# One rounding and one splitting instruction per weight slab in a 16-stage fp32 transformer block on one core

## The reference, cut to what matters

```python
mod  = silu(c) @ w_mod + b_mod                        # 2048 x 6144, for c and c_ctx
proj = hx @ w_in ; proj_c = hc @ w_in[:, k and v]     # 2048 x 8192, 256 tokens and 256 context tokens
...two attentions (differential with rope; neighbourhood)...
h    = h + gate * (concat(oa, ob) @ w_out)            # 2048 x 2048
proj = layernorm(rmsnorm(h)) @ w_in_2                 # 2048 x 7184: conv branch, q, k, v, o, gates
...conv gate, mLSTM cell...
h    = layernorm(ALPHA * h + mix @ w_out_2)
q    = h @ peer_wq ; top-16 of 128 keys twice, top-16 of 256 pairs
act  = gelu(h @ u.T)                                  # all 16384 experts, then masked to the chosen ones
ff   = (gate * act) @ v                               # 16384 x 2048
out  = layernorm(ALPHA * h + ff)
```

## Time and profile before

| | |
|---|---|
| median of 3 runs | 3272.75 us |
| profiled execution, first to last instruction | 3268.1 us |
| PE busy | 2988.1 us (91%) |
| DVE busy | 1825.0 us (56%), of it w_lo at L153 1264.5 us |
| ACT busy | 1490.0 us (46%), of it w_hi at L146 1145.7 us |
| loads | 944 x 512 KB, mean 159 GB/s |

### The profile page before, as it was taken

The page is one execution under the profiler, slowest core; times in us unless marked ns, Lnnn a source line. Parts: engine busy times, 40 slices in busy tenths (PEclk is TensorE's granted clock), DMA queues, the critical chain, the costliest instruction groups (busy, mean ns, idle before and its releaser), DMA issues. The chain is left out here.

```text
span 3268.1 us, 57214 instructions
## 1 busy us (share of the span) xinstructions
PE 2988.1 (91%) x17838; PEld 2617.1 (80%) x17838; DVE 1825.0 (56%) x3552; ACT 1490.0 (46%) x2793; POOL 173.1 (5%) x295
## 2 busy tenths in 40 slices
PE   6879996899886999969789999999996999999996
PEld 5668784788665999848789999999985788888885
DVE  5784235522456664455788844444459555555556
ACT  6663234422443444424344454444446455555553
POOL 0030001200000000010000000000018100000000
PEclk9999999899998999969899999999999999999998
DMA  6863231422343555516445555555540666666664
GB/s 238 289 217 120 95 124 34 142 96 97 103 154 118 166 182 180 177 39 210 148 148 184 181 182 183 180 180 184 182 141 0 211 193 193 193 192 193 193 193 135
DMA packets 139852, 520.38 MB, mean 159 GB/s; under 512 B 15760, under 2 KB 15792, under 8 KB 137488
## 3 DMA queue, kind: packets, MB, share of 16 engines
q1 hardware_dynamic: 136656, 500.25, 47.4%
q0 software_dynamic: 2560, 15.17, 1.4%
q10 hardware_dynamic: 576, 4.19, 0.3%
HBM read 515.35 MB, written 4.19 MB: 159 GB/s over the span
## 5 line engine op out<-in xcount | busy, mean ns | idle before, releaser
L153 DVE TENSOR_TENSOR w_lo<-raw,w_hi 128x512 fp32r<-128x512 f32 x1888 | 1264.5, 694 | 1224.4 <-ACT w_hi L146 1221.9
L146 ACT ACTIVATE w_hi<-raw 128x512 fp32r<-128x512 f32 x1888 | 1145.7, 630 | 971.6 <-PE PS L164 914.0
L162 PE MATMUL PS<-h_hi,w_hi 128*128 128x256 f32 x2944 | 834.1, 283 | 13.8 <-ACT L1729 8.6
L163 PE MATMUL PS<-h_lo,w_hi 128*128 128x256 f32 x2944 | 831.4, 282 | 0.0
L164 PE MATMUL PS<-h_hi,w_lo 128*128 128x256 f32 x2944 | 831.3, 282 | 0.0
L162 PEld LDWEIGHTS PS<-h_hi,w_hi 128*128 128x128 f32 x2944 | 564.9, 192 | 16.3 <-issue 10.8
L163 PEld LDWEIGHTS PS<-h_lo,w_hi 128*128 128x128 f32 x2944 | 564.7, 192 | 0.0
L164 PEld LDWEIGHTS PS<-h_hi,w_lo 128*128 128x128 f32 x2944 | 564.6, 192 | 0.0
L162 PE MATMUL PS<-w_hi,wj_hi 128*128 128x512 f32 x1024 | 399.2, 390 | 2.3 <-DVE wj_lo L1950 2.3
L163 PE MATMUL PS<-w_lo,wj_hi 128*128 128x512 f32 x1024 | 399.1, 390 | 0.0
L164 PE MATMUL PS<-w_hi,wj_lo 128*128 128x512 f32 x1024 | 398.9, 390 | 0.0
(11 more groups left out here) (318 smaller groups left out, 3116.0 us busy)
## 6 DMA issues: line engine op xcount, KB each, us to landing
raw<-in_u_s SPq DMA_DIRECT2D x256, 512.0 KB, 3.3
raw<-in_v SPq DMA_DIRECT2D x256, 512.0 KB, 4.7
raw<-in_w_in_s SPq DMA_DIRECT2D x112, 512.0 KB, 3.6
raw<-in_w_mod_s SPq DMA_DIRECT2D x96, 512.0 KB, 4.7
raw<-in_w_in_a SPq DMA_DIRECT2D x64, 512.0 KB, 3.5
raw<-in_w_in_b SPq DMA_DIRECT2D x64, 512.0 KB, 3.6
raw<-in_w_out_s SPq DMA_DIRECT2D x64, 512.0 KB, 4.2
raw<-in_wq_s SPq DMA_DIRECT2D x32, 512.0 KB, 3.2
```

The lines of the kernel that those rows point to most:

```text
L146: act.activation(w_hi[m % 2][:, half], raw[:, m % NRAW, half], ACT.Copy).then_inc(hi_ready, 1)
L153: dve.tensor_tensor(w_lo[m % 2][:, half], raw[:, m % NRAW, half], w_hi[m % 2][:, half].bitcast(F), ALU.subtract).then_inc(lo_ready, 1)
L162: pe.matmul(out, lhs[0], rhs[0], start=start, stop=False)
L163: pe.matmul(out, lhs[0], rhs[1], start=False, stop=False)
```

## The change

`round_slab` issues one ACT instruction for 1024 columns, after slab m-2 has been multiplied as a whole, and counts `hi_ready` by 2. `split_slab` issues one DVE instruction for 1024 columns after that, and counts `lo_ready` by 2. PE's code, the loads, the buffers and the order of slabs and other work on each engine are as before.

```diff
-        HALVES = [slice(0, SLAB // 2), slice(SLAB // 2, SLAB)]
...
         def round_slab(act, reg, m):
 
             raw_wait(act, (reg, m))
-            for x, half in enumerate(HALVES):
-
-                act.wait_ge(multiplied, halves(reg, m) + (x + 1))
-                act.activation(w_hi[m % 2][:, half], raw[:, m % NRAW, half], ACT.Copy).then_inc(hi_ready, 1)
+            act.wait_ge(multiplied, halves(reg, m) + 2)
+            act.activation(w_hi[m % 2][:, :], raw[:, m % NRAW, :], ACT.Copy).then_inc(hi_ready, 2)
 
         def split_slab(dve, reg, m):
 
-            for x, half in enumerate(HALVES):
-
-                dve.wait_ge(hi_ready, halves(reg, m) + (x + 1))
-                dve.tensor_tensor(w_lo[m % 2][:, half], raw[:, m % NRAW, half], w_hi[m % 2][:, half].bitcast(F),
-                                  ALU.subtract).then_inc(lo_ready, 1)
+            dve.wait_ge(hi_ready, halves(reg, m) + 2)
+            dve.tensor_tensor(w_lo[m % 2][:, :], raw[:, m % NRAW, :], w_hi[m % 2][:, :].bitcast(F),
+                              ALU.subtract).then_inc(lo_ready, 2)
```

## The result

| | before | after |
|---|---|---|
| median | 3271.93 us (4 runs, 3266.9 to 3275.98) | 3462.75 us (4 runs, 3457.53 to 3466.12) |
| span of the profiled execution | 3268.1 us | 3463.4 us |
| mean granted clock of TensorE | 0.965 | 0.965 |

The ratio is 1.0583, with an interval of 1.057 to 1.0596: slower by 5.8%, 190.8 us. The forecast was 3410, the range 3355 to 3472. So the sign and the range hold, but the sum of terms, 137, is 28% short. The range holds only because it was carried on to rival 1: the bounds of the prediction's own terms, 3365 to 3450, do not reach 3463.

A forecast was written before the change was run, and what follows sets the result against it. The prediction took PE, busy 91% of the span, as the bound. Its stall terms sum to 137 us, which with the profiled 3268.1 and 4.65 up to the median gave 3410 us, range 3355 to 3472.

The forecast's parts named there:

- rival 1: All chains 0.15 us longer, from a rounded output or two engines reading at once; 3468 us, chance 0.11.
- v, +38: v stage: wj_lo behind the even slab's split makes PE lose 0.30 us for each of 127 pairs, 38 us.
- u, +33: u stage: the Gelu ahead of the odd slab's rounding costs 0.26 us for 128 pairs, 33 us.
- q stages, q2 and k2, +12: These stages: a copy ahead of the rounding, as with the Gelu, loses 0.42 us for 32 pairs, 12 us.
- w_mod, +30: w_mod stage: two chains of 4.10 us per two slabs replace the DMA's pace; 80 slabs lose 30 us.
- Conv, +12: Conv part: DVE's 3.68 us block between two splits costs 1.5 us more at each of 8 places, 12 us.
- Chunk ends, +12: Where ACT or DVE reads PSUM between slabs, chains grow by 0.96 us at 8 places each; 12 us.
- A plain slab just fits, with 0.04 to spare: Slab with nothing else in its way: chain of 2.90 us against cover of 2.94, so no loss.
- "Nothing" for k and v of both attentions: k and v stages, slabs with context tokens: twice the cover, so no loss, 0 us.
- Rival 2: w_mod stage: TensorE's clock falls to 1.2 GHz, costing 35 us more; 3445 us, chance 0.10.
- Rival 3: All stages: the cover suffices, so no change; 3273 to 3279 us, chance 0.03.
- Rival 4: DVE and ACT: fewer fixed parts per instruction shorten PE's waits for w_lo, so faster; 3262 us, chance 0.04.

The follow-up runs named there:

- run 2: The changed kernel with wj(n+1) rounded and split between slabs 2n+1 and 2n+2 in the v stage; 3403.32 us, ratio 1.0403.
- run 3: The kernel before, with ACT rounding a slab in one instruction and DVE still splitting in two halves; 3370.33 us, ratio 1.0302.
- run 4: The kernel before, with DVE splitting a slab in one instruction and ACT still rounding in two halves; 3382.94 us, ratio 1.0344.
- run 5: The changed kernel with the Gelu behind the next rounding in the last 188 slabs of u; 3424.31 us, ratio 1.0471.
- run 6: The changed kernel with the 96 slabs of w_mod in two halves on ACT and DVE as before; 3424.88 us, ratio 1.048.
- run 1: The changed kernel with hi_ready and lo_ready counted by 1 for each slab instead of by 2; 3419.38 us, ratio 1.0449.
- run 8: The changed kernel counted by 1, with wj(n+1) between slabs in v and the Gelu behind the next rounding in u's last 188 slabs; 3352.88 us, ratio 1.0259.
- run 7: The kernel before, in halves, with ACT counting hi_ready by 2 for each half and DVE still counting by 1; 3270.11 us, ratio 1.0002.

## Why the prediction was right, and where it was short

- **Bound and mechanism: right.** PE was the bound, and DVE's and ACT's savings (97 and 149 us) brought nothing. The stalls sit where the text put them: wj_lo behind the split (runs 2 and 3), the Gelu ahead of the odd slab (runs 4 and 5), two chains in w_mod (run 6).
- **Durations: right.** ACT 1.06 and DVE 1.23 us. DVE's busy time fell by 97 us, not 150: the figure took 2 x 0.69 for two halves, though halves back to back take 1.29 together.
- **v, +38: measured +70.8. This is the term that was mis-sized most.** The chain was put at 3.24. Its links were taken from instructions that count by 1: 0.03 from the matmul's end to ACT and 0.04 from ACT to DVE. With the count by 2 they are 0.10 and 0.10, together 0.13 more (run 1). PE's start behind wj_lo came 0.14 after its end instead of 0.05, 0.09 more: the 0.05 was read behind w_lo. This link has nothing to do with the count, since its median is 0.13 in every kernel where the wait stalls PE, that of run 1 included, while behind w_lo it is 0.055 in all of them. PE has two waits in a row there, for `wj_split` and for `lo_ready`; whether that makes the difference was not tested. And behind a stall matmuls stand a little more than 0.227 apart for a while: from 2906.74 the last matmul before the next stall comes about 0.03 late. 0.30 + 0.13 + 0.09 + 0.03 = 0.55, measured 0.54, times 128 is 69.
- **u, +33: measured +46.4.** The same two links: run 1 takes 0.10 off a pair and 12.5 off the stage. What it leaves, +33.9 at 6.00 a pair, is the prediction's +33 at 6.02. So the term was right for the links that it took. They bring less than 0.13, since the Gelu's own wait begins the chain.
- **q stages, q2 and k2, +12: measured +15.7**, and +15.4 with the count of one, so here the links do not explain the difference. It stays open.
- **w_mod, +30: measured +31.3, with some luck.** The chain was put at 4.10 for two slabs. With the change it is 4.20, and 4.08 with the count of one, where the stage loses 27.3. So the chain was right for the links that it took, and a term 3 us too large met links that cost 4 more.
- **Conv, +12: measured +12.3**, and +13 with shorter links, so it is DVE's block, as worked out.
- **Chunk ends, +12: measured +12.5, with luck.** The row holds plain slabs too, which the prediction put at nothing: a pair in the gates rose from 5.49 to 5.62. If all 64 pairs of these stages lost as much it would be 8 us (an estimate, an upper bound), and with the count of one the row is at +4.5. The noise of w_out_2 comes on top.
- **"A plain slab just fits, with 0.04 to spare": right for the links that it took (run 8), wrong for the change.** With links 0.13 longer the chain is 3.03 against 2.94, and a plain pair loses 0.13 (run 2, and the gates). The margin of 0.04 was smaller than the error of the links.
- **"Nothing" for k and v of both attentions: right.** The +5.4 of the table is an effect of its cuts at DVE's splits. From PE's first matmul of k to its first of v it is 96.52 us before and 96.50 after in the first attention, 89.60 and 89.60 in the second; v takes 88.10 and 88.09, then 87.91 and 89.60, and this 1.7 stands in no other kernel.
- **The rivals.** Rival 1 had nearly the right time, 3468, by chains 0.15 longer; but the instructions kept their length, and it was the links between them that grew. That a count by 2 could lengthen them was in none of the cases. So the end of the range, which held the result, was right for a reason that did not occur. Rival 2: the clock stayed at its upper level from 66.5 us to the end of w_mod. Rivals 3 and 4 are out. The Trainium skill (Perfetto Trace Analysis, Optimizing Scalar/DVE Operations) pointed the right way: on engines at 56% and 46%, larger operations made bubbles on the third. Its other rule, that a large tile pays the latency once (VectorE: DVE Perf Modes, The TRN2 errata), also holds, 1.228 against 1.29 for the two halves, and was worth nothing, because DVE was not the bound.

## What to carry to other kernels

Halving an instruction on an engine that is half idle costs its fixed part there and buys slack for the engine behind it: before joining such halves, write down for each kind of stage the chain from the release of a buffer to its next use, with everything that stands ahead in each engine's order, and compare it with the work that the bound engine has in the mean time. A margin of 0.04 us was none here, with links read to 0.1; read the link times again from instructions of exactly the new form, the count on the semaphore included. Where a wide instruction is wanted all the same, move the other work out of the chain, behind it or between two of them (runs 2 and 5). Each taken alone, these two moves gave back 59 and 38 of the 191 us here, and the count by one 43; all three together gave back 110.

## What was not expected of the hardware

**An increment by 2 lengthens the wait before the instruction.** In the trace such an instruction is mostly preceded by a semaphore instruction of its own that holds its wait; with an increment by 1 the compute instruction mostly starts straight from the wait. Counted over all rounding and splitting instructions, with the median time from the releaser's end to the start:

```
kernel            ACT: own wait ahead / link      DVE: own wait ahead / link
before               102 of 1888 / 0.037 us           9 of 1888 / 0.032 us
after                820 of  944 / 0.097 us         901 of  944 / 0.102 us
count by one         108 of  944 / 0.037 us           2 of  944 / 0.033 us
halves, ACT by 2    1442 of 1888 / 0.097 us          10 of 1888 / 0.033 us
ACT whole, by 2      825 of  944 / 0.097 us           2 of 1888 / 0.033 us
DVE whole, by 2      104 of 1888 / 0.037 us         870 of  944 / 0.102 us
```

It follows the count in every kernel and neither the width nor the engine: 0.06 us on ACT, 0.07 on DVE. (A count by 2 on DVE's halves was not run.) The time goes with the separate instruction: in the kernel before, where all count by 1, the 80 roundings that have one ahead of them and wait for a matmul start 0.097 after its end, too, and the 1038 without one 0.037. In run 7 it was free, in the changed kernel it was 43 us. Whether the chip or the compiler asks for it these runs do not tell.

**A stall costs more than the wait that the profile shows.** Take the one in v above. The matmul ahead of it starts at 2906.11 and lasts 0.39, to 2906.50, though the next one could start at 2906.34. So of the 0.40 that PE stands still until 2906.74, 0.16 lies under a matmul that is still counted as busy, and the view shows a wait of 0.23. Then the first matmul lasts 0.49 instead of 0.39, and the next one comes 0.33 after it instead of 0.23: another 0.10, also busy time. The prediction had this second part from the earlier trace rows. In u every other stall is in no list of waits at all, since it ends before the matmul ahead of it does:

```profile
2112.21 0.28 PE L159 MATMUL PS<-h_hi,w_lo 128*128 128x256 f32 x1
2112.46 0.39 PE L157 MATMUL PS<-h_hi,w_hi 128*128 128x256 f32 x1
2112.68 0.28 PE L158 MATMUL PS<-h_lo,w_hi 128*128 128x256 f32 x1
```

The distances are 0.25 and 0.22, where 0.12 is usual: 0.23 us lost without an entry. In this way half of the loss stands in the profile as PE's busy time (+95 us); the list of waits alone would have shown 98 us of 191. What counts is the distance between the starts of matmuls.
